# Four of a conditioning projection's weight blocks moved from the latent attention to the start of the output projection

## The chip, the cores and the metric

The kernel runs on one core of a Trainium2 chip. The metric is the device time of one execution in microseconds (us); lower is better. Three executions of the kernel before took 2868.01 to 2868.85 us, median 2868.31 us.

## What is computed

One layer of a diffusion backbone over 128 context tokens and 512 latent tokens (640 in all), width 2048, all in float32. The part that matters here:

```python
mod = silu(cond) @ w_mod + b_mod            # (shift1, scale1, gate1, shift2, scale2, gate2)
h   = x * (1 + scale1) + shift1
z   = h @ w_in                              # feeds both attentions
o_na  = neighbourhood_attention(...)        # 8 heads x 128
o_mla = latent_attention(...)               # 8 heads
o   = concat(o_na, o_mla) @ w_o
x   = layernorm(ALPHA * x + gate1 * o)
x   = layernorm(ALPHA * x + gate2 * (silu(g) * u) @ w_down)   # g, u from x*(1+scale2)+shift2
```

`mod` is computed for two conditioning vectors (latent and context), so it is a product of a 2-row matrix with a 2048 x 12288 weight.

## The kernel before

**Precision.** A float32 product is made of three matmuls on rounded operands: every operand is split into a high part (ScalarE copies it, rounding) and a low part (VectorE subtracts the high part from the original). `mm3` (lines 1985 to 1987) issues high x high, high x low, low x high.

**One stream of weights.** SyncE loads weight blocks of 128 x 1024 values (512 KB) in one fixed order, `ORDER`, into the four slots of `raw`; the load of element p waits until element p-4 has been consumed (`stream_load`, line 623). An element is of one of two kinds. `("w", n)` is a block for TensorE: ScalarE writes `whi` (line 935), VectorE writes `wlo` (line 1385), and TensorE multiplies by them. `("m", m)` is a block of `w_mod`, which does not go through TensorE: VectorE multiplies it by one conditioning value for each partition and adds it to an accumulator (`gemv`, line 1413: four operations of 128 x 512, two for each conditioning vector). VectorE consumes both kinds in the order of the stream, each consumption counting on `lo_ready`.

**Units.** Eight consecutive modulation blocks make a unit u = m // 8, one accumulator. When its eighth block is in, TensorE sums the accumulator over partitions: `row_sums` for the gates (a row), `column_sums` (lines 2006 and 2007) for shifts and scales (columns; eight matmuls of two columns each for one unit), counted on `mred`. Units 9, 10 and 11 (blocks 72 to 95) are three quarters of scale2. Their accumulators `macc2` lie in the memory `acc`, which later holds the residual `xs`; so the residual may be loaded only after unit 11 is summed (`residual_in`, line 827: GpSimd waits `mred`, then issues four loads of 1280 KB, each after the one before has landed). Units 12 to 15 (gate2) accumulate elsewhere, from block 4 of the output projection on (`WO_MODS`).

**Latent attention.** Eight heads, `h` = 0 to 7, software-pipelined: TensorE makes the queries and keys of head h from one weight block, then scores and transposes by tile while the value product of head h-1 runs (line 2184), with softmax on VectorE and ScalarE between them (`stage`: maxima at lines 1503 to 1505, normalisation at line 1519). In each head VectorE does three modulation blocks: one before the low parts, one in two halves between them, one behind the last low part and ahead of tile 1's maxima (line 1680). GpSimd copies the values of the next head (`v_of_head`, line 764) once the product of the one before is done and its output is stored.

**Output projection.** 32 weight blocks (`B_WO + b`; called block b), four column chunks c of eight blocks; block b multiplies features 2q and 2q+1 (q = b % 8) for five token tiles: 30 matmuls. The attention output lies in DRAM (`oscr`), and in chunk 0 its 16 features are fetched by GpSimd's queue into three slots of `ostage` (line 840); ScalarE makes `oh` (line 1164) and VectorE `ol` (line 1687), and block b waits for `o_lo >= 2q + 2`. The same queue also stores the last head's output before feature 3 and, between features 3 and 4, loads the two 1024 KB broadcasts of `gate`. VectorE's order in iteration b of its loop is: features (0 to 3 at b = 0, then 2b+2 and 2b+3), at b = 7 the evacuation of chunk 0 with the residual, the low part of weight block b+2 (ScalarE's high part of it waits until TensorE is done with block b), then modulation blocks. The three column sums stand on TensorE's queue behind block 0; the residual's first load stands on GpSimd's queue behind feature 8; `mod2_parts` (four short operations on VectorE that use the sums) stands in iteration 2.

**Afterwards** come the layer norm, the feed-forward part (from 1160 us to the end) and the last layer norm.

Of the kernel before, what the change touches and what calls it, by code (L numbers as in the profile page):

```python
# [50 lines left out]
B_HEAD = B_VM + 4  # L51
# [16 lines left out]
    return [24 + 2 * (b - 8) + x for x in range(2)] if b < 12 else [64 + 2 * (b - 12) + x for x in range(2)]  # L68


def stream_order():

    order = [("w", n) for n in range(B_V + 2)]
    m = 0
    for b in range(16):
        order.append(("w", B_V + b + 2))
        order += [("m", m + x) for x in range(V_MODS[b])]
        m += V_MODS[b]
    for a in range(NH):
        for g in range(4):  # L80
            order += [("w", B_NA + 4 * a + g + 2), ("m", 32 + 8 * g + a)]
    for b in range(16):
        if B_KVL + b + 2 < B_QR:
            order.append(("w", B_KVL + b + 2))
        order += [("m", m) for m in lat_mods(b)]
    order += [("w", n) for n in range(B_QR, B_HEAD + 1)] + [("m", 72), ("w", B_HEAD + 1)]
    for h in range(NH):
        order += [("m", 72 + 3 * h + x) for x in range(0 if h else 1, 3)] + [("w", B_HEAD + h + 2)]
    m = 96
    for b in range(32):  # L90
        if b < 30:
            order.append(("w", B_WO + b + 2))
        order += [("m", m + x) for x in range(WO_MODS[b])]
        m += WO_MODS[b]
    return order
# [7 lines left out]
def reduces(u):  # L103

    return REDUCED.index(u) + 1
# [65 lines left out]
def build(nc, wstream, xT, xtok, cond, bmod, rpb, kcT, vc, ckvcT, krcT, lncol, lnrow, latg, bcol, rope, cap, ident, sel,  # L171
# [14 lines left out]
    with ctx:  # L186
# [512 lines left out]
        def _(pool):  # L699
# [134 lines left out]
            for k in range(KD):  # L834
                if k == 3:
                    head_out(2 * NH - 1)
                    pool.wait_ge(o_out, 16 * 2 * NH)
                if k >= 3:
                    pool.wait_ge(o_lo, k - 2)
                pool.dma_start(ostage[:, k % 3, :], oscr[k]).then_inc(o_in[k % 3], 16)  # L840
                if k == 3:
                    pool.wait_ge(grow_out, 64)
                    for c in range(2):

                        pool.dma_start(gate[:, c, :], modg[c:c + 1, 0:D].to_broadcast([P, D])).then_inc(gate_in, 16)
                if k == 8:

                    pool.wait_ge(mred, reduces(11))
                    residual_in(0)
            for c in range(1, 4):  # L850
                residual_in(c)
            for u in range(4, 8):
                gate_row_out(u)
# [516 lines left out]
        def _(dve):  # L1370
# [288 lines left out]
            for h in range(NH + 1):  # L1659
                if h:  # L1660
                    stage(None, NH + h - 1, 5, False)
                if h < NH:
                    if h:
                        gemv(None, 72 + 3 * h)

                    def low(j, dst, src, hi):

# [4 lines left out]
                    for r in range(2):  # L1672
                        k = slice(r * KEYS // 2, (r + 1) * KEYS // 2)
                        low(2 + r, kl_[:, k], ps[r][:, 0:KEYS // 2], kh[:, k])
                        gemv(None, 73 + 3 * h, (r,))
                    for s in range(5):
                        stage(None, NH + h, s, False)
                        if s == 0:
                            low(4, ql_[:, HT:T], ps[3][:, 0:HT], qh[:, HT:T])
                            gemv(None, 74 + 3 * h)  # L1680
                        if s == 1:
                            split(None, B_HEAD + h + 2)

# [34 lines left out]
            for b in range(32):  # L1718
# [27 lines left out]
                        own.link(ins)  # L1746
                if b < 30:
                    split(None, B_WO + b + 2)
                m = 96 + sum(WO_MODS[:b])
                for x in range(WO_MODS[b]):  # L1750
                    gemv(None, m + x)
                if b in WO_ROWS:
                    gate_row(4 + WO_ROWS.index(b), 4 + WO_ROWS.index(b) % 2)
                if b == 2:
                    mod2_parts()

            def s_sums(kk):
# [222 lines left out]
        def _(pe):  # L1980
# [404 lines left out]
            for b in range(31):  # L2385
# [27 lines left out]
                ins = tok_block(n, oh, ol, 2 * q, q == 0, q == 7, TOK_BANKS, before=before,  # L2413
                                after=(lambda t, ins: ins.then_inc(wo_done, 1)) if q == 7 else None)
                ins.then_inc(used, 1)
                if b == 0:
                    column_sums(range(9, 12), 6)
                if b in WO_ROWS:
                    u = WO_ROWS.index(b)
# [234 lines left out]
```

## Time and profile before

| what | value |
|---|---|
| median of three executions | 2868.31 us |
| the profiled execution's own time | 2868.85 us |
| its span in the profile | 2867.3 us |
| TensorE busy | 97% of the span |
| VectorE, ScalarE, GpSimd busy | 66%, 36%, 6% |
| mean granted TensorE clock | 0.986 of full |

The span is the time from the first to the last instruction in the profile, and 1.6 us of the execution's own time lie around it. "Busy" counts instructions that work; a wait is none. The granted clock is 1.00 at 2.4 GHz and 0.50 at 1.2 GHz.

### The profile page before, as it was taken

To read this page: it belongs to the slowest core of one execution; us is meant where nothing else is said; L and a number is where in the kernel's file an instruction comes from. 1 tells how busy PE (TensorE), PEld (TensorE's weight loads), DVE (VectorE), ACT (ScalarE), POOL (GpSimd) and SP (SyncE) were. 2 spreads that over 40 slices of the span, in tenths; PEclk is the share of its full clock that TensorE was granted. 3 is DMA by queue.
4 is the path that set the end of the run, shared out by engine and by line. 5 is a ranking of instruction groups with operands and counts; after the bars stand their busy time and mean duration, and the time that the engine had idled before them with its cause. 6 is when DMAs were issued, how large, how long until landed. Compare 5 with 4: busy or idle time off the path is not lost.

```text
span 2867.3 us, 42046 instructions
## 1 busy us (share of the span) xinstructions
PE 2794.2 (97%) x15817; PEld 2491.9 (87%) x15817; DVE 1892.5 (66%) x2941; ACT 1043.8 (36%) x1815; POOL 186.1 (6%) x258
## 2 busy tenths in 40 slices
PE   7899999999999998899999999999999999999997
PEld 2689999888888777899999999999999888888886
DVE  8766666586894887866666666666666555424338
ACT  7522333234553114644444444444444312112122
POOL 1121111000001000000000000000000000000005
PEclk9999999999999998899999999999999999999999
DMA  9754334362335745222222222222222535224232
GB/s 384 278 189 155 126 129 134 118 198 71 110 117 176 229 156 184 74 102 102 101 92 97 101 101 98 100 101 96 92 101 101 198 110 174 89 89 143 77 110 96
DMA packets 105768, 379.82 MB, mean 132 GB/s; under 512 B 14062, under 2 KB 14466, under 8 KB 103754
## 3 DMA queue, kind: packets, MB, share of 16 engines
q1 hardware_dynamic: 89664, 321.56, 32.4%
q0 software_dynamic: 15424, 56.87, 5.7%
q8 instruction: 62, 1.02, 0.1%
q14 instruction: 32, 0.26, 0.0%
q10 hardware_dynamic: 586, 0.12, 0.0%
HBM read 346.97 MB, written 33.48 MB: 133 GB/s over the span
## 4 chain that ended last, share of the span: by engine, by line
PE 90%; DVE 5%; DMA 3%; ACT 2%; issue 1%; SPq 0%; ACTq 0%; DVEq 0%
PE ps L1985 15%; PE ps L1986 15%; PE ps L1987 15%; PE ps L2483 12%; PE ps L2482 12%; PE ps L2484 12%; DMA mraw<-in_wstream 2%; PE ps L2184 1%; PE ps L2149 1%; PE ps L2132 1%; PE ps L2180 0%; DVE ps L1913 0%; DVE mlo L1436 0%; ACT stagef L1242 0%; PE ps L2007 0%
## 5 line engine op out<-in xcount | busy, mean ns | idle before, releaser
L2482 PE MATMUL ps<-actl,ringh 128*128 128x320 f32 x1408 | 435.4, 309 | 3.6 <-DVE ringl L1784 3.6
L2483 PE MATMUL ps<-acth,ringh 128*128 128x320 f32 x1408 | 435.1, 309 | 0.0
L2484 PE MATMUL ps<-actl,ringl 128*128 128x320 f32 x1408 | 435.1, 309 | 0.0
L2482 PE MATMUL ps<-acth,ringh 128*128 128x320 f32 x1056 | 327.4, 310 | 7.7 <-DVE ringl L1784 7.7
L2483 PE MATMUL ps<-actl,ringh 128*128 128x320 f32 x1056 | 327.1, 310 | 0.0
L2484 PE MATMUL ps<-acth,ringl 128*128 128x320 f32 x1056 | 327.1, 310 | 0.0
L1985 PE MATMUL ps<-dwh,fring 128*128 128x512 f32 x820 | 319.4, 390 | 1.0 <-DVE dwl L1888 0.9
L1987 PE MATMUL ps<-dwh,fring 128*128 128x512 f32 x820 | 319.1, 389 | 0.0
L1986 PE MATMUL ps<-dwl,fring 128*128 128x512 f32 x820 | 319.1, 389 | 0.0
L1888 DVE TENSOR_TENSOR dwl<-raw,dwh 128x1024 fp32r<-128x1024 f32 x82 | 100.4, 1224 | 291.4 <-ACT dwh L1341 291.4
L1784 DVE TENSOR_TENSOR ringl<-raw,ringh 128x512 fp32r<-128x512 f32 x264 | 181.7, 689 | 163.1 <-ACT ringh L1275 163.1
L1413 DVE SCALAR_TENSOR_TENSOR macc<-raw,conds,macc 128x512 f32<-128x512 f32 x390 | 270.4, 750 | 4.5 <-issue 1.2
L1385 DVE TENSOR_TENSOR wlo<-raw,whi 128x1024 fp32r<-128x1024 f32 x110 | 135.2, 1230 | 208.2 <-ACT whi L935 207.4
L2482 PEld LDWEIGHTS ps<-actl,ringh 128*128 128x128 f32 x1408 | 264.3, 188 | 4.4 <-DVE ringl L1784 4.4
L2484 PEld LDWEIGHTS ps<-actl,ringl 128*128 128x128 f32 x1408 | 264.3, 188 | 0.0
L2483 PEld LDWEIGHTS ps<-acth,ringh 128*128 128x128 f32 x1408 | 264.3, 188 | 0.0
L1275 ACT ACTIVATE ringh<-raw 128x512 fp32r<-128x512 f32 x264 | 166.7, 632 | 264.5 <-PE ps L2484 264.5
L935 ACT ACTIVATE whi<-raw 128x1024 fp32r<-128x1024 f32 x110 | 116.3, 1058 | 364.2 <-PE ps L1987 364.2
L1341 ACT ACTIVATE dwh<-raw 128x1024 fp32r<-128x1024 f32 x82 | 86.9, 1060 | 414.8 <-PE ps L1987 409.4
L2482 PEld LDWEIGHTS ps<-acth,ringh 128*128 128x128 f32 x1056 | 199.0, 188 | 8.1 <-DVE ringl L1784 8.1
L2483 PEld LDWEIGHTS ps<-actl,ringh 128*128 128x128 f32 x1056 | 199.1, 188 | 0.0
L2484 PEld LDWEIGHTS ps<-acth,ringl 128*128 128x128 f32 x1056 | 198.9, 188 | 0.0
(322 smaller groups left out, 5752.3 us busy)
## 6 DMA issues: line engine op xcount, KB each, us to landing
raw<-in_wstream SPq DMA_DIRECT2D x503, 512.0 KB, 3.7
mraw<-in_wstream SPq DMA_DIRECT2D x64, 512.0 KB, 7.7
fscr<-fst POOLq DMA_DIRECT2D x44, 320.0 KB, 2.4
fst<-fscr SPq DMA_DIRECT2D x21, 640.0 KB, 4.5
acc<-in_xT SPq DMA_DIRECT2D x8, 640.0 KB, 16.0
oscr<-ost POOLq DMA_DIRECT2D x16, 320.0 KB, 2.5
ostage<-oscr POOLq DMA_DIRECT2D x16, 320.0 KB, 4.2
acc<-in_xtok POOLq DMA_DIRECT2D x4, 1280.0 KB, 8.7
```

The costliest lines, as they stand in the source:

```text
L935: nc.scalar.activation(hi_of(n), raw[:, slot_of("w", n), :], ACT.Copy).then_inc(hi_ready, 1)
L1275: nc.scalar.activation(ring(ringh, (HALF * j + h) % 4), gu_source(u, half), ACT.Copy).then_inc(ghi, 1)
L1385: V.tensor_tensor(lo_of(n), raw[:, slot_of("w", n), :], hi_of(n).bitcast(f32), ALU.subtract).then_inc(lo_ready, 1)
L1413: ins = V.scalar_tensor_tensor(out=v, in0=w, scalar=f, in1=v, op0=ALU.mult, op1=ALU.add)
L1784: V.tensor_tensor(ring(ringl, s), gu_source(u, half), ring(ringh, s).bitcast(f32), ALU.subtract).then_inc(glo, 1)
L1888: V.tensor_tensor(lo, raw[:, d % 4, :], hi.bitcast(f32), ALU.subtract).then_inc(dlo, 1)
L1985: mm(out, ah, bh, start=first, stop=False)
L1986: mm(out, ah, bl, start=False, stop=False)
L1987: return mm(out, al, bh, start=False, stop=last)
L2482: mm(out, ringh[:, s, w], ah, start=first, stop=False, skip_group_check=True)
L2483: mm(out, ringh[:, s, w], al, start=False, stop=False, skip_group_check=True)
L2484: ins = mm(out, ringl[:, s, w], ah, start=False, stop=last, skip_group_check=True)
```

## The change

Blocks 72 to 83 stay as they were, three in each of heads 0 to 3. Heads 4 to 7 now take two each (84 to 91): the one behind the last low part is dropped. Blocks 92 to 95, the second half of unit 11, go one each into iterations 0 to 3 of the output projection, behind the low part of weight block b+2, in the stream as on VectorE. What needs unit 11 follows: the column sums of units 9 to 11 stand behind block 5 instead of block 0, `mod2_parts` in iteration 7 instead of 2, and the first load of the residual behind all 16 features instead of behind feature 8.

```diff
--- before.py
+++ after.py
@@ -68,6 +68,11 @@
     return [24 + 2 * (b - 8) + x for x in range(2)] if b < 12 else [64 + 2 * (b - 12) + x for x in range(2)]
 
 
+def head_mods(h):
+
+    return [72 + 3 * h + x for x in range(3)] if h < 4 else [84 + 2 * (h - 4) + x for x in range(2)]
+
+
 def stream_order():
 
     order = [("w", n) for n in range(B_V + 2)]
@@ -85,11 +90,13 @@
         order += [("m", m) for m in lat_mods(b)]
     order += [("w", n) for n in range(B_QR, B_HEAD + 1)] + [("m", 72), ("w", B_HEAD + 1)]
     for h in range(NH):
-        order += [("m", 72 + 3 * h + x) for x in range(0 if h else 1, 3)] + [("w", B_HEAD + h + 2)]
+        order += [("m", m) for m in head_mods(h)[0 if h else 1:]] + [("w", B_HEAD + h + 2)]
     m = 96
     for b in range(32):
         if b < 30:
             order.append(("w", B_WO + b + 2))
+        if b < 4:
+            order.append(("m", 92 + b))
         order += [("m", m + x) for x in range(WO_MODS[b])]
         m += WO_MODS[b]
     return order
@@ -843,11 +850,8 @@
                     for c in range(2):
 
                         pool.dma_start(gate[:, c, :], modg[c:c + 1, 0:D].to_broadcast([P, D])).then_inc(gate_in, 16)
-                if k == 8:
-
-                    pool.wait_ge(mred, reduces(11))
-                    residual_in(0)
-            for c in range(1, 4):
+            pool.wait_ge(mred, reduces(11))
+            for c in range(4):
                 residual_in(c)
             for u in range(4, 8):
                 gate_row_out(u)
@@ -1661,7 +1665,7 @@
                     stage(None, NH + h - 1, 5, False)
                 if h < NH:
                     if h:
-                        gemv(None, 72 + 3 * h)
+                        gemv(None, head_mods(h)[0])
 
                     def low(j, dst, src, hi):
 
@@ -1672,12 +1676,13 @@
                     for r in range(2):
                         k = slice(r * KEYS // 2, (r + 1) * KEYS // 2)
                         low(2 + r, kl_[:, k], ps[r][:, 0:KEYS // 2], kh[:, k])
-                        gemv(None, 73 + 3 * h, (r,))
+                        gemv(None, head_mods(h)[1], (r,))
                     for s in range(5):
                         stage(None, NH + h, s, False)
                         if s == 0:
                             low(4, ql_[:, HT:T], ps[3][:, 0:HT], qh[:, HT:T])
-                            gemv(None, 74 + 3 * h)
+                            if h < 4:
+                                gemv(None, head_mods(h)[2])
                         if s == 1:
                             split(None, B_HEAD + h + 2)
 
@@ -1746,12 +1751,14 @@
                         own.link(ins)
                 if b < 30:
                     split(None, B_WO + b + 2)
+                if b < 4:
+                    gemv(None, 92 + b)
                 m = 96 + sum(WO_MODS[:b])
                 for x in range(WO_MODS[b]):
                     gemv(None, m + x)
                 if b in WO_ROWS:
                     gate_row(4 + WO_ROWS.index(b), 4 + WO_ROWS.index(b) % 2)
-                if b == 2:
+                if b == 7:
                     mod2_parts()
 
             def s_sums(kk):
@@ -2413,7 +2420,7 @@
                 ins = tok_block(n, oh, ol, 2 * q, q == 0, q == 7, TOK_BANKS, before=before,
                                 after=(lambda t, ins: ins.then_inc(wo_done, 1)) if q == 7 else None)
                 ins.then_inc(used, 1)
-                if b == 0:
+                if b == 5:
                     column_sums(range(9, 12), 6)
                 if b in WO_ROWS:
                     u = WO_ROWS.index(b)
```

## Rows read from the trace of the kernel before

**Rows 1.** Part 4 of the profile page, whole kernel.
```profile
PE 90%; DVE 5%; DMA 3%; ACT 2%; issue 1%; SPq 0%; ACTq 0%; DVEq 0%
```

**Rows 2.** Busy time by stretch: start and end us, length, PE, PEld, DVE, ACT, POOL; clock; DMA.
```profile
509.40:519.80 10.40, 10.40 (x42) 9.63 (x43) 0.19 (x1) 0.00 (x0) 0.00 (x0) 0.51 0.02 9
...
721.10:724.50 3.40, 1.34 (x11) 1.08 (x11) 3.26 (x10) 1.32 (x5) 0.00 (x0) 1.00 0.49 154
724.50:727.90 3.40, 3.23 (x16) 2.83 (x14) 3.16 (x14) 1.70 (x6) 0.00 (x0) 0.52 0.50 157
...
886.00:889.00 3.00, 1.66 (x14) 1.50 (x13) 1.95 (x3) 2.81 (x6) 0.00 (x0) 1.00 0.14 50
895.60:898.60 3.00, 3.00 (x29) 2.96 (x27) 2.05 (x2) 1.16 (x2) 0.54 (x1) 1.00 0.99 371
898.60:908.90 10.30, 10.30 (x36) 9.04 (x37) 1.65 (x2) 1.47 (x2) 1.96 (x3) 0.50 0.72 261
```

**Rows 3.** Chain of waits, heads 2 to 4 of the latent attention: start us, us, what.
```profile
762.24 4.29 PE ps L2184 x10
...
783.57 4.29 PE ps L2184 x10
...
805.34 4.29 PE ps L2184 x10
```

**Rows 4.** Timeline, head 4: start us, us, engine, line, what.
```profile
805.38 2.73 DVE L1413 SCALAR_TENSOR_TENSOR acc<-raw,conds,acc 128x512 f32<-128x512 f32 x4
...
811.35 0.49 DVE L1503 TENSOR_REDUCE mx<-ps 128x1 f32<-128x320 f32 x1
...
812.00 0.84 POOL L764 COPY vh<-vm 128x768 f32<-128x768 f32 x1
...
812.28 0.58 DVE L1505 TENSOR_TENSOR mx<-mx 128x1 f32<-128x1 f32 x1
```

**Rows 5.** Timeline, head 2.
```profile
768.40 0.84 POOL L764 COPY vh<-vm 128x768 f32<-128x768 f32 x1
...
769.18 0.16 DVE L1505 TENSOR_TENSOR mx<-mx 128x1 f32<-128x1 f32 x1
```

**Rows 6.** Timeline, TensorE, blocks 0 to 2 of the output projection.
```profile
895.64 0.28 PE L2006 MATMUL ps<-unit,acc 128*128 128x2 f32 x2
...
902.95 0.77 PE L1985 MATMUL ps<-whi,oh 128*128 128x512 f32 x1
...
912.67 0.39 PE L1985 MATMUL ps<-whi,oh 128*128 128x512 f32 x1
```

**Rows 7.** Timeline, VectorE, features 3 to 5; in brackets idle before and its releaser.
```profile
895.74 0.83 DVE L1687 TENSOR_TENSOR ol<-ostage,oh 128x640 fp32r<-128x640 f32 x1 [6.39 <-ACT oh L1164]
...
903.26 0.82 DVE L1687 TENSOR_TENSOR ol<-ostage,oh 128x640 fp32r<-128x640 f32 x1 [5.05 <-ACT oh L1164]
905.32 0.83 DVE L1687 TENSOR_TENSOR ol<-ostage,oh 128x640 fp32r<-128x640 f32 x1 [1.23 <-ACT oh L1164]
```

**Rows 8.** Issues of DMAs from 893 to 905 us: KB each, median us to landing.
```profile
gate<-modg POOLq DMA_DIRECT2D x2, 1024.0 KB, 7.1
ostage<-oscr POOLq DMA_DIRECT2D x4, 320.0 KB, 8.9
```

**Rows 9.** Timeline, ScalarE and VectorE, blocks 4 to 6.
```profile
940.13 1.06 ACT L935 ACTIVATE whi<-raw 128x1024 fp32r<-128x1024 f32 x1 [4.48 <-PE ps L1987]
...
945.02 1.55 DVE L1687 TENSOR_TENSOR ol<-ostage,oh 128x640 fp32r<-128x640 f32 x2
...
946.93 1.06 ACT L935 ACTIVATE whi<-raw 128x1024 fp32r<-128x1024 f32 x1 [1.69 <-PE ps L1987]
```

**Rows 10.** Timeline, a residual load, the end of block 7's evacuation, block 9.
```profile
948.72 0.86 POOL L831 DMA_DIRECT2D acc<-in_xtok  x1 [8.53 <-DMA acc<-in_xtok]
...
956.42 3.07 DVE L1745 BATCH_NORM_STATS2 stat<-acc 128x6 f32<-128x512 f32 x5
...
960.79 0.50 PE L1985 MATMUL ps<-whi,oh 128*128 128x512 f32 x1 [0.23 <-DVE wlo L1385]
```


## Prediction

> **What bounds the kernel now.** I read four views, from coarse to fine. The page first: the chain that ended last runs over TensorE for 90% of the span [rows 1], so an edit counts by what it does to TensorE: its waits, and the rate at which it works. Next the busy time by stretch, for the granted clock: the reader is to see that the three column sums run at full clock until 898.6 and then the array is at 0.50 until 908.9, ten microseconds in which it is busy throughout and does half the work [rows 2]. Then the chain of waits through the heads, for the length of a head. Last the timelines of two heads and of the first output blocks, where the moved work leaves and arrives. The terms below are against the profiled execution's own 2868.85 us, which is 0.54 above the median of 2868.31. I call indistinguishable what lies within 0.2%, or 5.7 us, of the median, about what a measurement of this kernel can tell.
>
> **Work that only moves.** The four blocks cost VectorE 2.73 each [rows 4], in both places; their loads are the same four, 512 KB each. The 24 column-sum matmuls and the four operations of mod2_parts are the same too. Nothing is saved on an engine's total. What changes is who waits.
>
> **Heads 4 to 7: a gain of 1.7.** Removing 2.73 from VectorE ahead of tile 1's maxima looks like much, but what follows does not start sooner by that. The maxima of the next tile begin at 811.35 [rows 4], right behind the scores that TensorE has by then; VectorE would only idle before them. What does move is a collision. At 812.28 a maximum of 128 x 1 takes 0.58 instead of 0.16: it ends when GpSimd's copy of 0.84, begun at 812.00, ends [rows 4]. In head 2 VectorE was a little earlier, since its dropped-to-be block starts a unit and is cheaper; there the copy began at 768.40, 6.16 after the value product's start instead of 6.66, and the same maximum took 0.16 [rows 3, 4, 5]. That head lasted 21.33 (783.57 - 762.24), the next 21.77 (805.34 - 783.57) [rows 3]. So the price of the collision is 0.44, and a head without it exists in this trace. With the block gone the copy can begin no earlier than in head 2, since it waits for the value product, and that is enough. 4 heads x 0.44 = 1.8; I take 1.7. Bounds: 0, if the copy only slides into another operation; 2.5, if the last head's longer tail gains as well. The rest of the way is cover: no queue waits for the dropped block, and SyncE's loads only come earlier.
>
> **Blocks 0 and 1: a cover is taken away.** Between block 0's last matmul at 895.64 and block 1's first at 902.95 stand the column sums [rows 6]. Behind their cover the features come in late: feature 3's low part ends at 895.74 + 0.83 = 896.57, feature 5's at 905.32 + 0.83 = 906.15 [rows 7]. Without the sums block 1 can start at 896.65, a wait of 1.0. It lasts as long as a full-rate block, 6.81 (30 matmuls; the distance of two ScalarE releases in rows 9 is 6.80), and ends at 903.5. Block 2 needs feature 5 at 906.15: 2.7 more. That feature is late because of DMA: four loads of features took a median of 8.9 in this stretch, behind two gate loads of 1024 KB [rows 8], with the DMA engines 0.99 busy at 371 GB/s [rows 2]. The change adds to it. Block 94's load goes out when block 92 is consumed, 945.02 - 940.13 = 4.9 after ScalarE's release [rows 9], at 895.9 + 4.9 = 900.8; there SyncE's queue had nothing to issue before. Its 0.52 MB at 371 GB/s is 1.4. Sharing with GpSimd's queue it may push feature 5 back by 0 to 1.4; I take 0.8. Together 1.0 + 2.7 + 0.8 = **4.5**, bounds 3.7 and 5.2.
>
> **The clock after that wait: 0.9.** TensorE would idle some 3.5 ahead of block 2. The trace has two stretches to set beside it. From 721.1 to 724.5 the array was busy for 1.34 of 3.4, and the clock fell for the 3.4 that followed: 1.7 lost. From 886 to 889 it was busy for 1.66 of 3.0, and it did not fall [rows 2]. The wait lies nearer the first but is framed by dense blocks, so I take half of 1.7. Bounds 0 and 3.4.
> The Trainium skill, page "TensorE: Matmul & The Clock Gate", section "Why this matters for your kernels", says that an idle gap of about this size between bursts puts the clock back to half rate. By that rule the term is the full 1.7 and my sum is 0.8 higher; the row at 721.1 agrees, though its gap held some work.
>
> **The column sums behind block 5: minus 0.9.** They stood from 895.64 to 902.95 [rows 6], 3.0 of it at full and 4.3 at half clock, so 5.2 of full-rate work, and this is paid in both versions. (The sums, block 1's 6.81 and the 5.1 lost make 17.1; the rows have 912.67 - 895.64 = 17.0.) The question is the half clock. Before, it lasted 10.3, so 5.1 was lost. The sums of units 4 to 7 came behind a dense stretch, as these will now, and were followed by 10.4 at half clock, 5.3 lost [rows 2]. So the new place protects them from nothing. The fall comes some time into the sums and the rise only after the blocks behind them have run for a while; how much of the sums it catches is chance. I take 4.2 lost, between these two rows and the 1.7 of the shorter stretch at 724.5. Against 5.1 that is -0.9; bounds -5.1 (no fall) and +0.2.
>
> **Iterations 1 to 4: hidden, by little.** VectorE's iteration now holds a low part, a modulation block and two features. Blocks 4 and 5 have that already: ScalarE is released at 940.13, the features are done at 945.02 + 1.55 = 946.57, the next release is at 946.93 [rows 9]. The cover is a block's 6.81, and 0.3 of it is left; if it goes, each further 1 of delay is 1 on TensorE, at three blocks. The late one would be the second feature, whose load GpSimd issues when VectorE is done with the third before it. That is some 6 after a release (4.9, a low part of 0.83, and the issue), and its low part is due 6.8 + 4.9 + 0.8 = 12.5 after it, its high part 0.74 before: 5.8 for the load. I cost it at 0, bounds 0 and 3.
>
> **The residual: 0.** Its first load leaves after the sums instead of at 907. GpSimd's wait for one such load was 8.53 and the issue 0.86 [rows 10], so it lands about 9.4 behind the sums. VectorE comes for it after block 6 (6.8) and a high and a low part (4.9 - 2.7 = 2.2), at 9.0, later if block 6 runs in part at half clock. Anything late shows: behind chunk 0's evacuation (its statistics end at 959.5) the low part for block 9 is already the last to come, 0.23 of idle [rows 10]. The moved mod2_parts comes after that low part and is under 1. The removed load frees DMA time between 907 and 916. I take 0, bounds 0 and 1.5.
>
> **Sum.** -1.7 + 4.5 + 0.9 - 0.9 + 0 + 0 = +2.8 on the profiled 2868.85, or 2871.1 from the median.
>
> **The rivals.**
> *The feature loads become the bound (slower).* With modulation blocks in blocks 1 to 4, SyncE loads 1.05 MB for each block and GpSimd 0.66, or 250 GB/s over 6.81, and a feature load that takes over 6 makes TensorE wait in each of blocks 3 to 5. For it: the 8.9 of rows 8 and the 0.3 left in rows 9. Against it: the gates are through by then, and the residual's load is gone. At the 8.9 of rows 8 the wait is up to 2.8 a block; with half of that over three blocks, 4.2, the sum is +7.0: 2875.3. It decides from 7 a load, where 3 more make the sum leave the 5.7. Chance 0.13.
> *No half clock at the sums.* Block 0's sums fell behind a thin stretch, blocks 0 to 5 are dense. If that was the cause, 5.1 comes back: +2.8 - 4.2 = -1.4: 2866.9. Against it stands 509.4 to 519.8. Chance 0.12.
> *The full gain (faster).* As before, and the features come in time as well, so that neither the wait nor its clock is paid: -1.7 - 5.1 + 1.0 = -5.8: 2862.5. The loads before feature 5 would have to take half their time. Chance 0.04.
> *It doesn't do anything that can be seen.* The heads gain nothing, the wait is short, the half clock falls as before: between -1 and +1 in all, 2868.3. The collision has no twin but head 2. Chance 0.11.
> The forecast itself has 0.60, with a range of its own from 2869 to 2874.
>
> **How the numbers follow.** The prediction is 2871.0. The range from 2866.0 to 2875.5 takes in the forecast, the null, most of the no-half-clock case and most of the loads case, and leaves out the far ends of both and the full gain, some 0.15. Every case but the slow loads and the full gain lies within 5.7 of the median (2862.6 to 2874.0); of the loads case about 0.10 lies above, and of the forecast 0.03, if both clock terms come out high. So faster 0.04, same 0.83, slower 0.13. Wherever the sums lie, the moment of the half clock near the layer norm may shift as well, by a microsecond either way; that is in the range.
>
> **What the new profile would show.** Heads 4 to 7: 21.3 each between value products, and line 1505 at 0.16 beside the copy; if it stays 0.58, the first term is wrong. Block 1 starts 1.0 after block 0's end, released by line 1687; block 2 waits 2.7 to 4.1 for the same line; if it doesn't, feature 4's and 5's loads took less than I read. Column sums behind block 5 with a clock of 0.50 within them; if it stays 1.00, rival two holds. Waits of blocks 3 to 5 for line 1687 would speak for rival one. Block 7's evacuation on VectorE starts right behind the low part, or waits for the residual. What would make the whole wrong is a stretch at half clock longer than any here, or a wait in the heads that I have not seen.

## The result and the profile after

The changed kernel takes 2875.35 us (median of 20 runs, 2868.36 to 2879.76), the kernel before 2868.78 (20 runs, 2867.30 to 2870.00). The ratio is 1.0022 with a 95% interval of 1.0015 to 1.0029: 6.6 us slower, just beyond the 5.7 that I had called indistinguishable, and clear of this measurement's noise. It lies 4.4 above my forecast of 2871.0, outside the 2869 to 2874 that I gave the forecast itself, and within my range (2866.0 to 2875.5) by 0.15: nine of its 20 runs lie above the range, so that the median stays inside is luck. Its runs spread over 11 us where those of before spread over 2.7. The profiled run took 2876.83, with a span of 2875.3 against 2867.3: 8.0 are to be found in it.

Functions are inserted ahead, so lines have moved: the value product is L2191 (before L2184), the maxima L1507 to L1509 (L1503 to L1505), the first of an output block's three products L1992 (L1985), the column sums L2013 and L2014, a feature's low part L1692 (L1687). The page, part 4 (answers to [rows 1]):

```profile
PE 87%; DVE 6%; DMA 3%; ACT 2%; issue 1%; POOL 0%; SPq 0%; ACTq 0%; DVEq 0%; POOLq 0%
```

TensorE's share fell and VectorE's rose, but that says little: the fastest kernel below has 88% and 6%. New is GpSimd with its queue (POOL, POOLq). POOLq stands in the row of just those kernels here in which TensorE waits for a feature ahead of block 1 or 2.

**The heads** came out as forecast. First the chain of waits with the value products of heads 3 to 5 (answers to [rows 3]); then the timeline inside head 4 (answers to [rows 4]):

```profile
783.35 4.29 PE ps L2191 x10
...
790.29 0.60 DVE mx L1509
...
805.12 4.29 PE ps L2191 x10
...
826.45 4.29 PE ps L2191 x10
```

```profile
811.26 0.84 POOL L771 COPY vh<-vm 128x768 f32<-128x768 f32 x1
...
812.06 0.16 DVE L1509 TENSOR_TENSOR mx<-mx 128x1 f32<-128x1 f32 x1
```

Head 3 keeps its three modulation blocks, lasts 21.77 (805.12 - 783.35) and still has the collision (0.60). Head 4 is thinned, lasts 21.33 (826.45 - 805.12), and the copy starts 6.14 behind the value product (811.26 - 805.12) where it had started 6.66 behind it; in head 2 of before it was 6.16 [rows 3, 4, 5]. The maximum takes 0.16. Head 3 beside head 4 is a control within one trace. Block 0 of the output projection starts 1.9 earlier, 0.2 of it an earlier start of the whole stretch, so the heads gave 1.7.

**The output projection** gave back more. TensorE's timeline, the blocks that waited and the column sums (answers to [rows 6]; in brackets the idle before and its releaser):

```profile
886.86 0.47 PE L1992 MATMUL ps<-whi,oh 128*128 128x512 f32 x1 [1.33 <-DVE ol L1692]
...
895.90 0.47 PE L1992 MATMUL ps<-whi,oh 128*128 128x512 f32 x1 [2.00 <-DVE ol L1692]
...
906.95 0.77 PE L1992 MATMUL ps<-whi,oh 128*128 128x512 f32 x1 [3.97 <-DVE ol L1692]
...
936.95 0.28 PE L2013 MATMUL ps<-unit,acc 128*128 128x2 f32 x2
...
944.66 0.77 PE L1992 MATMUL ps<-whi,oh 128*128 128x512 f32 x1
...
968.11 0.50 PE L1992 MATMUL ps<-whi,oh 128*128 128x512 f32 x1 [0.36 <-DVE wlo L1389]
```

Blocks 1 and 2 each waited for a feature's low part, 2.00 and 3.97. The first product of block 2 takes 0.77 instead of 0.47: the clock had fallen. Busy time by stretch (columns as in [rows 2]; of block 1, of the wait, of block 2, and of the sums at their new place):

```profile
896.00:903.00 7.00, 6.99 (x30) 5.43 (x30) 3.76 (x5) 0.00 (x0) 0.54 (x1) 1.00 0.98 359
```

```profile
902.20:905.40 3.20, 0.79 (x4) 0.32 (x2) 0.82 (x1) 0.92 (x2) 0.00 (x0) 1.00 0.82 335
905.50:912.30 6.80, 5.35 (x13) 4.23 (x14) 6.17 (x8) 2.76 (x4) 1.54 (x3) 0.50 0.64 203
936.90:939.60 2.70, 2.70 (x26) 2.66 (x25) 1.30 (x2) 1.68 (x2) 0.00 (x0) 0.99 0.61 211
939.60:949.80 10.20, 10.20 (x37) 9.14 (x37) 4.05 (x6) 0.74 (x1) 0.88 (x1) 0.50 0.61 194
```

TensorE was at 1.2 GHz (0.50) for 6.8, 5.35 of it at work, so 2.7 of full-rate work was lost on block 2: the blocks 2 to 5 take 936.95 - 906.95 = 30.0, which is four times 6.81 and 2.7 more, with no other wait among them (block 4 came close: its second feature was ready at 923.04, its first matmul started at 923.18). The sums then met the same half clock behind block 5 as they had behind block 0: 10.2 long, 5.1 lost.

Why the features were late shows on GpSimd's queue and in the DMA issues from 893 to 906 (answers to [rows 8]):

```profile
891.01 0.54 POOL L847 DMA_DIRECT2D ostage<-oscr  x1 [3.15 <-DMA oscr<-ost]
892.00 1.07 POOL L852 DMA_DIRECT2D gate<-modg  x2 [0.45 <-issue]
893.07 1.08 POOL L847 DMA_DIRECT2D ostage<-oscr  x2
```

```profile
ostage<-oscr POOLq DMA_DIRECT2D x4, 320.0 KB, 10.7
gate<-modg POOLq DMA_DIRECT2D x1, 1024.0 KB, 9.6
```

Feature 3's load leaves at 891.01. It does not read the last head's output, but it stands behind that output's store in the queue, and GpSimd waited 3.15 for the store. The next two stand behind two gate loads of 1024 KB in the same queue and land after a median of 10.7 (before 8.9). VectorE's low parts of features 3, 4 and 5 (answers to [rows 7]) then decide when blocks 1 and 2 start:

```profile
894.93 0.82 DVE L1692 TENSOR_TENSOR ol<-ostage,oh 128x640 fp32r<-128x640 f32 x1 [7.49 <-ACT oh L1168]
...
904.57 0.82 DVE L1692 TENSOR_TENSOR ol<-ostage,oh 128x640 fp32r<-128x640 f32 x1 [4.81 <-ACT oh L1168]
905.98 0.83 DVE L1692 TENSOR_TENSOR ol<-ostage,oh 128x640 fp32r<-128x640 f32 x1 [0.58 <-ACT oh L1168]
```

VectorE was idle 7.49 and 4.81 ahead of them: neither it nor the modulation work that it now does there was what TensorE waited for; it waited for the features to land. Feature 5 is done at 906.81. TensorE was through with block 0 at 893.75 (886.86 and the 6.89 that it took before), 1.9 earlier than before, so against TensorE the feature came 2.55 later than before (906.81 - 906.15 + 1.89): 1.0 by the store, 1.5 by the loads. Block 94's load on SyncE's queue, which I had made answerable for that, is not shown to have a part in it. The first gate load already took 6.87 for 6.09 and landed at 898.88, before that load left at 899.79; and in two kernels below that have no such load, feature 5's took 11.66 (heads alone) and 11.00 (late sums), for 11.59 here and 10.04 before. What makes the two gate loads slower stays open.

The account of the profiled run: heads -1.9 with the earlier start, waits ahead of blocks 1 and 2 +6.1 (2.15 counted from 893.75, and 3.97), clock behind the wait +2.7, sums 0, from block 0 to block 9 together 81.25 for 72.04 (+9.2, of which 0.4 is small pieces), and 0.7 much later: 8.0. From block 9 up to 2272 the matmuls come 7.3 later than before (7.1 to 7.6). The 0.7 arises in the last part, the feed-forward's down projection, where a block waits that did not wait before:

```profile
2273.01 0.50 PE L1992 MATMUL ps<-dwh,fring 128*128 128x512 f32 x1 [0.81 <-DVE dwl L1895]
```

A weight load ahead of it took 5.87 where it had taken 5.06. The change edits nothing there, and what slowed the load is not shown.

### The profile page after: what moved, and what is told of

It reads as the page before. It is cut to its first block, busy times and chain, and to the rows that moved or that the text cites. A ratio compares the mean times of both kernels' runs of the same rounds, so it can differ in the third digit from the quotient of the medians.

```text
span 2875.3 us, 42046 instructions
## 1 busy us (share of the span) xinstructions
PE 2797.1 (97%) x15817; PEld 2493.7 (87%) x15817; DVE 1889.7 (66%) x2941; ACT 1043.5 (36%) x1815; POOL 185.5 (6%) x258
## 4 chain that ended last, share of the span: by engine, by line
PE 87%; DVE 6%; DMA 3%; ACT 2%; issue 1%; POOL 0%; SPq 0%; ACTq 0%; DVEq 0%; POOLq 0%
PE ps L1992 15%; PE ps L1994 15%; PE ps L1993 15%; PE ps L2491 12%; PE ps L2489 12%; PE ps L2490 12%; DMA mraw<-in_wstream 2%; PE ps L2191 1%; PE ps L2156 1%; DVE ps L1920 1%; PE ps L2139 1%; DVE acc L1922 1%; DVE stat L1970 0%; PE ps L2187 0%; DMA ostage<-oscr 0%
## 5 line engine op out<-in xcount | busy, mean ns | idle before, releaser
L1992 PE MATMUL ps<-dwh,fring 128*128 128x512 f32 x820 | 319.4, 389 | 1.8 <-DVE dwl L1895 1.8
```

The costliest lines, as they stand in the source:

```text
L1992: mm(out, ah, bh, start=first, stop=False)
```

## The experiments

Times are medians; each ratio is against runs of the kernel before on the same chip (medians 2869.1 to 2869.4).

**Does the lost cover cost this without the moved blocks?** Kernel before, all blocks in the heads; only sums, the residual's first load and mod2_parts move:

```
-                if k == 8:
-                    pool.wait_ge(mred, reduces(11))
-                    residual_in(0)
-            for c in range(1, 4):
+            pool.wait_ge(mred, reduces(11))
+            for c in range(4):
...
-                if b == 2:
+                if b == 7:
                     mod2_parts()
...
-                if b == 0:
+                if b == 5:
                     column_sums(range(9, 12), 6)
```

> The kernel before with what hangs on unit 11 moved as in the change (column sums behind block 5, the residual's first load behind all features, mod2_parts in iteration 7), while all 24 modulation blocks stay in the heads. Theory: the loss comes from the cover that the sums gave to features 3 to 5, so it appears in full: waits of 1 to 2 and 3 to 4 ahead of blocks 1 and 2, 1.7 to 2.7 of half clock after them, no gain in the heads: 2868.8 + 7 to 9 = 2876 to 2878, slower than the changed kernel by the heads' 1.7. Rival (the moved blocks' loads and VectorE work are the cause): near the kernel before plus 1 to 3, 2870 to 2872.

Measured 2874.68 (11 runs, 2871.25 to 2879.57), 1.0020 [1.0011, 1.0029]: 5.5 slower, under the forecast of 7 to 9. Its profiled run happened to be its fastest, 2871.25:

```profile
896.28 0.47 PE L1982 MATMUL ps<-whi,oh 128*128 128x512 f32 x1 [0.93 <-DVE ol L1684]
...
906.79 0.47 PE L1982 MATMUL ps<-whi,oh 128*128 128x512 f32 x1 [3.43 <-DVE ol L1684]
```

```profile
906.50:912.00 5.50, 5.21 (x23) 4.33 (x24) 2.93 (x4) 1.60 (x3) 1.65 (x4) 1.00 0.81 264
```

Both waits are there, with no modulation block near. They come with the moved sums, and the theory that the moved loads cause them falls. Beside the 8.3 of the change (6.6 and the heads' 1.7) the 5.5 leaves 2.8, which the two intervals (2.0 and 2.6 either way) neither give to the moved blocks nor deny them. The clock did not fall behind a wait of 3.43 in this run, and the sums lost about 1.9, at a half clock of 3.4 (27.9 from the first sum to block 9, less 5.2 for the sums, three blocks of 6.81 and 0.36 of wait), not 5.1. Slower runs of the same kernel lie up to 8 above it.

**The heads alone.** Kernel before with blocks 92 to 95 left out, their loads too; a quarter of the second layer's scale vector is then incomplete.

```
+def head_mods(h):
+    return [72 + 3 * h + x for x in range(3)] if h < 4 else [84 + 2 * (h - 4) + x for x in range(2)]
...
-                        gemv(None, 72 + 3 * h)
+                        gemv(None, head_mods(h)[0])
```

> The heads' part alone: the kernel before, in which heads 4 to 7 do two modulation blocks each, and blocks 92 to 95 are left out of the computation altogether (a quarter of scale2 is incomplete; their loads are left out too). Theory: four heads of 21.3 instead of 21.8, 1.7 faster: 2868.8 - 1.7 = 2867.1, and nothing else moves. Rival (the collision only slides elsewhere): no gain, 2868.8. Rival (VectorE's 2.7 for each head counts in full): 10.9 faster, 2857.9.

Measured 2868.06 (11 runs), 0.9995 [0.9986, 1.0005]: -1.1 to -1.4, not to be told from nothing by the time alone. The chain of waits, heads 4 and 5:

```profile
804.68 4.29 PE ps L2190 x10
...
826.02 4.29 PE ps L2190 x10
```

21.34 a head (826.02 - 804.68): the 1.7 is in the trace.

**Take the gate loads from between the features.** After, with both gate loads behind all 16 feature loads:

```
-                if k == 3:
-                    pool.wait_ge(grow_out, 64)
-                    for c in range(2):
...
+            pool.wait_ge(grow_out, 64)
+            for c in range(2):
```

> The changed kernel with one edit: the two 1024 KB loads of gate stand behind all 16 feature loads on GpSimd's queue instead of between features 3 and 4. Theory (the late features 4 and 5, uncovered by the move of the column sums, are most of the loss): block 2 no longer waits for feature 5, so its wait of 4.0 and the 2.7 lost at half clock after it go; block 1 still waits some 2 for feature 3, which comes before the gates. 2875.4 - 6.7 = 2868.7, within 1 of the kernel before. Rival (the loads of the moved modulation blocks crowd the queue): the wait for feature 5 shrinks by no more than 1, 2874 to 2875. Rival (half clock at the sums is dearer in the new place): the wait goes, but the total stays above 2872.

Measured 2871.98 (11 runs, 2868.31 to 2874.49), 1.0007 [0.9998, 1.0016]. Block 2's wait is gone, block 1's is not, and now the clock falls behind that one:

```profile
895.79 0.47 PE L1991 MATMUL ps<-whi,oh 128*128 128x512 f32 x1 [1.98 <-DVE ol L1691]
```

```profile
896.60:900.00 3.40, 3.40 (x10) 2.62 (x9) 3.40 (x6) 0.82 (x2) 0.00 (x0) 0.50 0.69 243
```

The gate loads carry about half of the excess. What is left is feature 3, ahead of which no gate stands: it waits for the last head's store. That wait I had foreseen, and the fall of the clock behind it not, so the time came 3.3 above the 2868.7 that I expected.

**Take both delays away.** After, with feature 3's load ahead of the last head's store, and one gate load each ahead of features 10 and 12. The sums stay together behind block 5.

```
-                if k == 3:
+                if k == 4:
                     head_out(2 * NH - 1)
+                if k == 10:
                     pool.wait_ge(o_out, 16 * 2 * NH)
+                if k in (10, 12):
+                    pool.wait_ge(grow_out, 64)
+                    c = (k - 10) // 2
+                    pool.dma_start(gate[:, c, :], modg[c:c + 1, 0:D].to_broadcast([P, D])).then_inc(gate_in, 16)
...
-                if k == 3:
-                    pool.wait_ge(grow_out, 64)
-                    for c in range(2):
...
```

> The changed kernel with the late features made early and nothing else: feature 3 is loaded as soon as its slot is free, ahead of the store of the last head's output instead of behind it (the store goes behind feature 3, its wait ahead of feature 10), and gate's two loads go one each ahead of features 10 and 12, where the queue is idle. The three units' sums stay together behind block 5. Theory (the loss is these waits and the half clock behind them, 6.1 + 2.7): both waits go, and what is left of the change is the heads' gain, with the half clock at the sums as before: 2869 - 1.7 = 2867.3. Rival (the moved blocks or the sums' new place cost by themselves): 2870 or more, with waits at blocks 3 to 5 or more half clock behind block 5.

Measured 2867.31 (11 runs, 2865.77 to 2870.42), 0.9994 [0.9985, 1.0003]: 8.0 faster than after, and under before by what the heads give (1.85, though the interval takes in no difference). The two stretches, before the sums and from the sums on:

```profile
885.00:931.00 46.00, 44.37 (x208) 36.29 (x206) 29.64 (x40) 17.03 (x24) 8.60 (x16) 1.00 0.76 258
931.00:943.00 12.00, 12.00 (x51) 10.86 (x51) 5.21 (x7) 1.19 (x2) 0.87 (x1) 0.57 0.59 190
```

No wait at blocks 1 and 2, no fall of the clock ahead of the sums; the sums keep theirs. Block 5 waited 0.30 for a feature. The profiled run was the slowest of the eleven (2870.42), and the half clock that starts at 509.5 in after's profile starts at 512.1 in this one, so that most of its 3.1 above the median probably lies ahead of all this. The run closes the account of the change: within what such medians tell, everything that it cost was the late features. Which part of their lateness the moved blocks' loads had is not taken apart by it.

**What brings the half clock to the sums?** After, with the sums of units 9 and 10 behind block 0 and unit 11 behind block 5:

```
-                if b == 5:
-                    column_sums(range(9, 12), 6)
+                if b == 0:
+                    column_sums(range(9, 11), 6)
+                if b == 5:
+                    column_sums(range(11, 12), 6, 2)
```

> The changed kernel with the column sums of units 9 and 10 back behind block 0, and only unit 11's behind block 5. Theory: 3.6 of sums again cover the wait for features 3 to 5. Block 1's wait of 2.0 goes, block 2's shrinks from 4.0 to some 2.5; together 3.6 less. Behind block 5 only eight matmuls of two columns are left, 1.8, like unit 8's alone in the attention, after which the clock stayed at 1.00; so the 5.2 lost there comes back, while the half clock behind block 0 may be caught by more of the sums (up to 2.4 more lost). 2875.4 - 3.6 - 5.2 + 0 to 2.4 = 2866.6 to 2869. Rival (half clock comes from the place, not from the length of the thin stretch): only the 3.6, 2871.8.

Measured 2866.81 (11 runs), 0.9991 [0.9982, 1.0000].

```profile
896.00:905.00 9.00, 9.00 (x36) 7.61 (x36) 4.61 (x6) 0.83 (x1) 0.54 (x1) 0.62 0.98 356
928.00:940.00 12.00, 12.00 (x62) 10.11 (x61) 8.41 (x12) 4.83 (x6) 2.49 (x4) 1.00 0.77 228
```

Sixteen thin products in a row behind block 0 brought a fall, and covered the features again (blocks 1 and 2 didn't wait); the eight behind block 5 brought none. Then one unit's eight behind each of blocks 0, 1 and 5:

```
-                if b == 5:
-                    column_sums(range(9, 12), 6)
+                if b in (0, 1, 5):
+                    n = (0, 1, 5).index(b)
+                    column_sums(range(9 + n, 10 + n), 6, n)
```

> The changed kernel with the three units' column sums spread: unit 9 behind block 0, unit 10 behind block 1, unit 11 behind block 5, eight matmuls or 1.8 each; gate's loads stay between features 3 and 4. Theory (the half clock follows a long thin stretch, not the place): no half clock at any of the three. Block 1 waits some 0.3 for feature 3, block 2 some 2 for feature 5, and that wait together with 1.8 of sums before it may still bring the clock down for 3.4 to 6.8. 2866 to 2869, about the same as with units 9 and 10 together. Rival (any column sums bring the clock down): 2870 or more.

Measured 2868.57 (11 runs), 0.9996 [0.9987, 1.0005]. No fall at any of the three, but waits of 0.35 and 2.23 at blocks 1 and 2, and a fall behind the second:

```profile
904.60:911.50 6.90, 4.80 (x11) 3.80 (x12) 6.16 (x9) 3.05 (x4) 1.08 (x2) 0.53 0.60 201
936.00:946.00 10.00, 10.00 (x54) 8.54 (x53) 5.34 (x7) 2.96 (x4) 0.88 (x2) 1.00 0.80 269
```

**Both together, which went wrong.** The spread sums with the gate loads behind all features (the two diffs above):

> As the one with the sums spread, and gate's two loads behind all features. Theory: neither waits nor half clock are left from block 0 to block 7. Against the kernel before: heads -1.7, half clock of block 0's sums -5.1, wait for feature 3 +0.3: 2869 - 6.5 = 2862.5. Rival (half clock comes anyway): 2866 to 2868.

Measured 2871.66 (11 runs), 1.0009 [1.0000, 1.0018]: a miss of 9. Blocks 0 to 7 ran as I expected, at full clock. GpSimd's queue, and then TensorE's timeline:

```profile
931.21 1.06 POOL L851 DMA_DIRECT2D gate<-modg  x2
933.91 0.88 POOL L838 DMA_DIRECT2D acc<-in_xtok  x1 [1.64 <-PE ps L2013]
948.66 0.87 POOL L838 DMA_DIRECT2D acc<-in_xtok  x1 [13.87 <-DMA acc<-in_xtok]
```

```profile
949.24 0.47 PE L1991 MATMUL ps<-whi,oh 128*128 128x512 f32 x1 [1.86 <-DVE tmp L1734]
...
960.03 0.79 PE L1991 MATMUL ps<-whi,oh 128*128 128x512 f32 x1 [2.10 <-DVE wlo L1388]
```

The gate loads run beside the residual's first load, which takes 14.5 from issue to landing, where the changed kernel's took 7.1; the evacuation is late, blocks 8 and 9 wait, and a fall of the clock follows each wait. I had moved the collision, not removed it. The same with the sums of units 4 to 7 spread too, one unit ahead of each of tiles 0 to 3 of the first low-rank block:

```
-                            if t == 3:
+                            if t == 0:
...
-                                column_sums(range(4, 8), 7)
+                            if t < 4:
+                                column_sums(range(4 + t, 5 + t), 7, t)
```

> As the one with the sums spread and gate late, and the other long column sums of the kernel, those of units 4 to 7 ahead of the last token tile of the low-rank projection's first block, are dealt out too: one unit ahead of each of tiles 0 to 3, so 1.8 of thin work between 1.4 of dense work. Theory: if it is the share of dense work that matters, the fall at 509 goes, which cost 5.3 there: 2862.5 - 5.3 = 2857. Rival (1.4 of dense work between them is too little): the fall stays, 2862 to 2863, perhaps earlier in the block.

Measured 2866.18 (11 runs), 0.9986 [0.9977, 0.9995]: 5.5 under the run above it, a second site's half clock gone, and the same collision still in it (waits of 1.61 and 3.44, a fall of the clock behind the second). I had expected 2857, since I built on the 2862.5 that did not come. This profile also has what the others lack, a half clock right behind a lump of eight: 1.1 into block 1, which had waited 0.33 for feature 3 behind unit 9's sums:

```profile
891.50:894.90 3.40, 3.40 (x9) 2.63 (x9) 3.40 (x7) 0.59 (x1) 0.00 (x0) 0.50 0.75 247
```

The other way round, kernel before with the three sums behind blocks 0, 1 and 2, the gate loads behind all features, mod2_parts in iteration 4, and the residual's first load still behind feature 8:

```
-                if b == 0:
-                    column_sums(range(9, 12), 6)
+                if b in (0, 1, 2):
+                    n = (0, 1, 2).index(b)
+                    column_sums(range(9 + n, 10 + n), 6, n)
```

> The kernel before, all 24 modulation blocks in the heads, with the sums spread (unit 9 behind block 0, 10 behind block 1, 11 behind block 2), gate's loads behind all features, and mod2_parts in iteration 4. Theory: the change's own moved blocks are not needed for the gain behind block 0. Half clock -5.1, nothing in the heads: 2869 - 5 = 2864, slower by the heads' 1.7 than the same with the blocks moved. Rival (the moved blocks add waits in blocks 2 to 5): it is as fast as that one or faster.

Measured 2874.96 (11 runs), 1.0021 [1.0012, 1.0030]: a miss of 11. GpSimd's queue, TensorE:

```profile
914.24 0.88 POOL L831 DMA_DIRECT2D acc<-in_xtok  x1 [14.55 <-PE ps L2006]
```

```profile
926.59 0.77 PE L1984 MATMUL ps<-whi,oh 128*128 128x512 f32 x1 [5.69 <-DVE ol L1686]
```

The residual's load may go only when the last sums are read. At the head of GpSimd's queue it waited 14.55 for them, with the loads of features 9 and up behind it, and block 4 waited 5.69. Block 9 waited 2.52 as well.

**The version that follows.** After, the sums spread at both sites, the gate loads one each ahead of features 10 and 12, where the features behind them have time to spare:

> As the kernel with the sums spread at both sites, with gate's loads one each ahead of features 10 and 12 instead of behind feature 15. Theory (late gates delayed the residual's first load from 8.7 to 13.9, which made waits of 1.6 and 3.4 ahead of blocks 8 and 9, and half clock): those 5 and their half clock go, 2866.5 - 6 = 2860 to 2861. Rival (the residual is late for another reason): no faster than 2865.

Measured 2858.97 (7 runs, 2857.87 to 2862.14), 0.9967 [0.9956, 0.9979]. And with feature 3's load ahead of the last store as well:

> As the one with gate's loads between the features, and feature 3's load ahead of the last head's store. Theory: block 1's wait of 0.3 goes, and with it the half clock that it and unit 9's sums brought together in one profile (1.7): 2858 to 2860, the fastest version. Rival: no difference.

Measured 2858.78 (6 runs, 2858.56 to 2860.41), 0.9966 [0.9954, 0.9978]: 10.4 under the kernel before, the fastest here, though not to be told from the one before it.

```profile
480.00:1100.00 620.00, 608.42 (x3119) 508.21 (x3117) 470.24 (x883) 213.50 (x470) 38.59 (x62) 1.00 0.47 151
509.40:519.80 10.40, 10.40 (x57) 8.96 (x57) 3.07 (x7) 1.80 (x4) 0.00 (x0) 1.00 0.08 18
```

The granted clock is 1.00 over 620 us, and the stretch at 509.4 shows 57 matmul records where it showed 42 [rows 2]. Last, what the change itself is worth once its costs are gone: the same kernel with all 24 blocks back in the heads (the sums then behind blocks 0, 1 and 2):

```
-                if b < 4:
-                    gemv(None, 92 + b)
```

> As the one before it, but with all 24 modulation blocks in the heads as in the kernel before; units 9, 10 and 11 are summed behind blocks 0, 1 and 2, the residual's first load stands behind all features. Theory: what the change itself is worth once nothing is uncovered is the heads' 1.7, so this is 1.7 slower: 2860 to 2862. Rival (the moved blocks cost in blocks 1 to 4): equal or faster.

Measured 2861.23 (8 runs, 2859.66 to 2861.92), 0.9972 [0.9962, 0.9983]: 2.4 slower than with the change. In the profile the thinned heads take 21.34 and the full ones 21.75, four times 0.41, or 1.6. The other 0.8 lies ahead of the heads, where the two kernels do the same work: at the value product of 735.2 the profile with all blocks is already 0.77 behind, with a half clock at 718.6 that the other profile does not have.

## Why the prediction came out as it did

**Heads, -1.7: right,** in size and cause. The copy starts earlier, the maximum drops to 0.16, and head 3 beside it shows the old price. The Trainium skill, page "SBUF — State Buffer", section "Who interferes with whom", says that a VectorE instruction with two inputs in SBUF contends with a GpSimd instruction that reads SBUF, and that the ports which they share are an exclusive lock. The trace of before agrees: the maximum's 0.58 ended at 812.86, the copy at 812.84 [rows 4].

**Waits ahead of blocks 1 and 2, 4.5: cover right, size 1.6 short.** Block 0's sums had been the cover of features 3 to 5. I had 4.5 and 6.1 came: 1.0 of the difference is GpSimd's longer wait for the last head's store (3.15, in before 2.14), which delays feature 3 and all behind it, and 0.7 is that the loads delayed feature 5 by 1.5, where I had taken 0.8 of a possible 1.4. That 0.8 stood for block 94's load, and that cause is not shown: feature 5's load took that long in kernels without it (11.66 and 11.00). I had taken feature 3's moment from before and put no bound on its store, so the result lies above my upper end of 5.2. That the lateness is the loss is shown from both sides: without it the changed kernel takes 2867.31, and with it, but without the moved blocks, the kernel before takes 2874.68.

**Clock after that wait, 0.9: too low, 2.7 in the profiled run.** The row at 721.1 gave the right kind, but its half clock lasted 3.4; here it lasted 6.8. Nor was its 1.7 a price in time, since VectorE is busy there for 3.26 and 3.16 of 3.40 [rows 2]: from the value product at 573.5 to the one at 740.3 the profiles with that half clock take 166.4 to 166.9, those without it 166.1. I had halved the term; with the full 1.7 the sum would have been +3.6, still short. The Trainium skill, page "TensorE: Matmul & The Clock Gate", section "Why this matters for your kernels", has a plain rule, that an idle gap of a few microseconds between bursts puts the clock back. The trace agrees at block 2 (3.97). The runs show more than the rule, though: the clock stayed at 1.00 behind a wait of 3.43 (before with late sums) and behind the 2.00 at block 1 of after, and fell behind 1.98 in the kernel with late gates: a wait of one size went either way. With loads that vary, a kernel that has such waits may draw its clock anew each run. That fits the changed kernel's spread of 11 us. Each run's mean granted clock is known: the two fastest (2868.36 and 2869.03) have 0.989, the slowest (2879.76) 0.985, and 0.004 of 2870 is some 11 us of full-rate time. The mean does not say where the clock fell, so that it was behind these waits is argued.

**Sums behind block 5, -0.9: 0 came.** 10.2 at half clock for 10.3. "The new place protects them from nothing" was right and should have been the value; the 0.9 was hope without a row. What protects them is another neighbour: eight at a time between dense blocks, the clock stayed up through every lump in the profiles, and fell soon behind two of 38, each time at a wait of TensorE (0.33 and 2.23).

**Iterations 1 to 4 and the residual, 0 and 0: right.** Blocks 3 to 5 show no wait for a feature, but of the 0.3 that I saw left there 0.14 was, at block 4. The residual's first load landed 7.1 after its issue, and block 9's wait went from 0.23 to 0.36. The rival that the feature loads become the bound had its number near the result (2875.3), and not its mechanism: it had the waits in blocks 3 to 5. The rival without a half clock at the sums, and with it the full gain, fall for the changed kernel.

**The step that failed** is thus the size of the waits with their clock: 5.4 forecast, 8.8 measured. These 3.4 are the most of the 5.2 by which the profiled run's +8.0 lies above my +2.8; 0.9 is the sums behind block 5, and 0.7 belongs to no term, it is the weight load in the feed-forward part. That all my bounds' upper ends together made +13, and that the terms are tied (a later feature makes a longer wait, and behind a wait the clock may fall), should have put more than 0.13 on "slower". The half clock is not the longer for a longer wait, though: it lasted 6.8 at 2.23 (sums spread) and 3.4 at 5.69 (before with spread sums).

**The longer wait for the store** needs no theory of the heads. GpSimd's issues of DMAs over the store of the last head's output, first in the changed kernel (887.3 to 890.8), then in the kernel before (889.2 to 891.7):

```profile
q8 instruction: 1, 0.02, 2.3%
oscr<-ost POOLq DMA_DIRECT2D x1, 320.0 KB, 3.4
```

```profile
oscr<-ost POOLq DMA_DIRECT2D x1, 320.0 KB, 2.4
```

In the changed kernel one packet of 16 KB of the queue that the profile calls instruction (q8) runs beside the store, from 887.80 for 1.30; in the kernel before it had come at 886.69, ahead of the store. So it is in all eleven profiles with the store ahead of feature 3: seven have the packet within the store, which then takes 3.0 to 3.7, and four have it elsewhere, and there the store takes 2.4 (before, late sums, before with spread sums, and the thinned kernel with the gates between features). No run moved the packet alone.

**What stays open.** What makes the gate loads and the features behind them land later than in before, and what decides which waits the clock follows.

## What to carry to other kernels

Before moving a piece of filler work, ask what arrives during it: the time that it occupies may be the only cover of a late load, and the trace shows that as operands that end just as the filler does. A transfer that is due late and stands in a queue ahead of one that is due early costs twice, in the wait and in the clock behind it; move it to where nothing is due on either side, and look what it then meets (here the residual's load). Many thin matmuls in one lump cost more than their own time; cut into small lumps between dense work, and with no wait behind them, they cost what they last.

## What the runs showed of the hardware

- TensorE was busy for all of a stretch and still fell to 1.2 GHz: 24 to 32 matmuls of two columns in a row (each shows as two records) brought 10.2 to 10.4 at half clock, 5.1 to 5.3 lost; in one profile (late sums) it was 3.4, with 1.9 lost. Sixteen in a row did it as well (0.62 over 9.0). In 38 lumps of eight the clock never fell within one, and it fell soon behind two, each time at a wait. Lumps of eight at both sites were worth 8.5 together (2867.31 to 2858.78).
- A TensorE wait of 2 to 4 may or may not be followed by a fall (1.98 yes, 2.00 no, 3.43 no, 3.97 yes), and the half clock behind it lasted 3.4 to 6.8.
- Feature loads of 320 KB took a median of 10.7 around two loads of 1024 KB in GpSimd's queue; with those two moved away, the loads of features 4 and 5 took 4.1 and 4.3. The residual's first load of 1280 KB took 7.1 in the changed kernel and 14.5 beside the two.
- The last head's store of 320 KB took 2.4, and 3.0 to 3.7 where a 16 KB packet of the instruction queue ran beside it.
